# Score blocks issued one step later, norm factors spread by rounded products of ones, low diagonals on ScalarE in two places, second latent sum inside the next slab

## The reference, cut to what matters

```python
def rms_norm_2(x, g):
    y = xf * lax.rsqrt(jnp.mean(xf * xf, axis=-1, keepdims=True) + EPS)
    return (y * g.astype(jnp.float32)).astype(x.dtype)

def hgrn2_recurrence(q, k, v, log_f):
    ...
    b = jnp.cumsum(log_f, axis=3)
    q_in = q * jnp.exp(b)
    k_in = k * jnp.exp(-b)
    k_out = k * jnp.exp(b_last - b)
    scores = jnp.einsum('nbhtk,nbhsk->nbhts', q_in, k_in)
    scores = jnp.where(causal, scores, 0.0)
    o_intra = jnp.einsum('nbhts,nbhsv->nbhtv', scores, v)
    def step(state, inp):
        q_n, k_n, v_n, dec_n = inp
        o_inter = jnp.einsum('bhtk,bhkv->bhtv', q_n, state)
        state = state * dec_n[..., None] + jnp.einsum('bhsk,bhsv->bhkv', k_n, v_n)
        return state, o_inter
    ...

def hgrn2_branch(hq, hf, hi, hz, lb, hg_norm_g):
    f = lb + (1.0 - lb) * jax.nn.sigmoid(hf.astype(jnp.float32))
    q = jax.nn.silu(hq.astype(jnp.float32)).reshape(B, S, HG_HEADS, HG_DIM)
    ...
    o = rms_norm_2(o, hg_norm_g)
    o = o * jax.nn.silu(hz).reshape(B, S, HG_HEADS, HG_DIM)
    return o.reshape(B, S, HG_WIDTH)

def mla_branch(cq, ckv, kr, mz, q_a_g, w_uq, kv_a_g, w_ukv):
    q = (rms_norm_2(cq, q_a_g) @ w_uq).reshape(B, S, MLA_HEADS, QK_DIM)
    ...
    kv = (rms_norm_2(ckv, kv_a_g) @ w_ukv).reshape(B, S, MLA_HEADS, QK_NOPE + V_DIM)
    ...
```

## Time and profile before

| | |
|---|---|
| median of 3 runs | 1286.68 us |
| the profiled execution | 1286.33 us |
| its span | 1284.5 us |
| TensorE busy | 1272.7 us, 99% of the span |
| VectorE busy | 751.1 us, 58% |
| ScalarE busy | 692.7 us, 54% |
| GpSimd busy | 498.1 us, 39% |
| granted TensorE clock | 0.999 of full speed |

### The profile page before, as it was taken

One profiled execution on the slowest core, in us unless ns is written; L12 is line 12 of the kernel. 1 busy time (PEld: TensorE's weight loads), 2 busy tenths in 40 slices (PEclk: granted clock), 3 DMA queues, 4 the chain that ended last, 5 costly groups with the idle time before them and its releaser, 6 DMA issues.

```text
span 1284.5 us, 16123 instructions
## 1 busy us (share of the span) xinstructions
PE 1272.7 (99%) x6217; PEld 1063.7 (83%) x6217; DVE 751.1 (58%) x1361; ACT 692.7 (54%) x1047; POOL 498.1 (39%) x207
## 2 busy tenths in 40 slices
PE   9999999999999999999999999999999999999998
PEld 7888888888887888888888888888888888888886
DVE  6656556552138356565668388888757556642442
ACT  5535544542235657666447578878655545462422
POOL 4453433434444332322345633343433333234530
PEclk9999999999999999999999999999999999999999
DMA  5732232324333232332143322222223222326411
GB/s 183 268 122 94 90 98 87 98 92 164 96 102 98 76 107 78 97 98 65 58 157 112 115 82 67 81 72 78 83 82 101 84 78 75 96 94 206 163 58 66
DMA packets 42588, 132.30 MB, mean 103 GB/s; under 512 B 6992, under 2 KB 9744, under 8 KB 42000
## 3 DMA queue, kind: packets, MB, share of 16 engines
q1 hardware_dynamic: 36416, 115.36, 28.5%
q10 hardware_dynamic: 6096, 15.92, 3.5%
HBM read 124.97 MB, written 10.49 MB: 105 GB/s over the span
## 4 chain that ended last, share of the span: by engine, by line
PE 83%; DVE 8%; ACT 6%; issue 2%; DMA 1%; POOL 0%; SPq 0%; ACTq 0%; DVEq 0%
PE banks L516 25%; PE banks L518 25%; PE banks L517 25%; PE banks L723 2%; PE banks L715 1%; PE banks L704 1%; ACT whi L1113 1%; DVE hd L2017 1%; DVE ylo L1783 1%; PE banks L630 1%; DMA raw<-w 1%; DVE hs L1984 1%; PE banks L965 1%; DVE nfull L1779 1%; ACT L1403 0%
## 5 line engine op out<-in xcount | busy, mean ns | idle before, releaser
L506 POOL TENSOR_TENSOR wlo<-raw,whi 128x1024 fp32r<-128x1024 f32 (+2 forms) x198 | 487.1, 2462 | 714.4 <-ACT whi L1113 714.2
L516 PE MATMUL banks<-hhi,whi 128*128 128x512 f32 x736 | 293.6, 399 | 0.2 <-DVE hlo L1830 0.2
L518 PE MATMUL banks<-hlo,whi 128*128 128x512 f32 x736 | 287.4, 390 | 0.0
L517 PE MATMUL banks<-hhi,wlo 128*128 128x512 f32 x736 | 287.1, 390 | 0.0
L1113 ACT ACTIVATE whi<-raw 128x1024 fp32r<-128x1024 f32 (+2 forms) x198 | 205.3, 1037 | 144.3 <-PE banks L518 77.7
L516 PE MATMUL banks<-yhi,whi 128*128 128x512 f32 x432 | 170.6, 395 | 0.2 <-DVE ylo L1783 0.2
L518 PE MATMUL banks<-ylo,whi 128*128 128x512 f32 x432 | 168.3, 390 | 0.0
L517 PE MATMUL banks<-yhi,wlo 128*128 128x512 f32 x432 | 168.2, 389 | 0.0
L518 PEld LDWEIGHTS banks<-hlo,whi 128*128 128x128 f32 x736 | 138.2, 188 | 30.0
L516 PEld LDWEIGHTS banks<-hhi,whi 128*128 128x128 f32 x736 | 138.3, 188 | 26.0 <-DVE hlo L1830 1.0
L517 PEld LDWEIGHTS banks<-hhi,wlo 128*128 128x128 f32 x736 | 138.6, 188 | 24.7
(11 more groups left out here) (407 smaller groups left out, 2258.6 us busy)
## 6 DMA issues: line engine op xcount, KB each, us to landing
raw<-w SPq DMA_DIRECT2D x193, 512.0 KB, 3.6
rel_tab<-relx ACTq DMA_DIRECT2D x1, 4096.0 KB, 20.1
tab<-rel_tab SPq DMA_DIRECT2D x16, 224.0 KB, 3.5
x<-xt ACTq DMA_DIRECT2D x1, 2048.0 KB, 9.3
x_kept<-x ACTq DMA_DIRECT2D x1, 2048.0 KB, 7.3
parts_kept<-mcg SPq DMA_DIRECT2D x8, 256.0 KB, 4.4
mgt<-parts_kept SPq DMA_DIRECT2D x8, 256.0 KB, 3.9
x<-x_kept ACTq DMA_DIRECT2D x1, 2048.0 KB, 10.5
```

What stands on the lines that cost most here:

```text
L506: nc.gpsimd.tensor_tensor(lo[:, begin:width], raw[:, n % 2, begin:width], f32(hi[:, begin:width]), ALU.subtract).then_inc(lo_done, 1)
L516: nc.tensor.matmul(dst, a[0], b[0], start=first, stop=False)
L517: nc.tensor.matmul(dst, a[1], b[0], start=False, stop=False)
L518: return nc.tensor.matmul(dst, a[0], b[1], start=False, stop=last)
```

## The change

The matrix of ones is kept once, rounded (`wones`). A factor is split into a high and a low part (`fhi`, `flo`), each makes a diagonal (`split_diagonal`), and TensorE multiplies `wones` by both, two float32r products in place of one float32 product. The diagonals are written into tiles that are free at that time. In the attention's norm and the second block's norm ScalarE makes the low diagonal in four instructions (`low_diagonal`); elsewhere VectorE does. For the latents the second pair of products moves into the pa slab that follows, and the low half of the rotated keys to the end of VectorE's part. In the recurrence the score blocks 1 and half of 3 are issued one step later (k 6 in place of 5), block 0 too (7 in place of 6); the product `hqb` moves behind `hg_sum` on VectorE, and its high half (`hg_scaled`) behind `hg_low` and the cut on ScalarE.

```diff
@@ norms
+            def split_diagonal(done, factor, hi, lo=None):
+                n = factor.shape[1]
+                V.tensor_copy(fhi[:, 0:n], factor).then_inc(done.did("rhi"), 1)
+                dve.wait_ge(done.sem, done.at("rhi"))
+                V.tensor_tensor(flo[:, 0:n], factor, f32(fhi[:, 0:n]), ALU.subtract).then_inc(done.did("rlo"), 1)
+                diagonal(hi, f32(fhi[:, 0:n])).then_inc(done.did("diag"), 1)
+                if lo is not None:
+                    dve.wait_ge(done.sem, done.at("rlo"))
+                    diagonal(lo, flo[:, 0:n]).then_inc(done.did("diaglo"), 1)
...
+            def low_diagonal(to):
+                for t in range(TT):
+                    last = nc.scalar.activation(to[:, t * P:(t + 1) * P], ident, ACT.Copy, scale=flo[:, t:t + 1])
+                return last
...
@@ TensorE, attention's norm (the others alike)
-                            nc.tensor.matmul(bank[3], ones, adiag, start=True, stop=True).then_inc(nbP.did("wide"), 1)
+                            nc.tensor.matmul(bank[3], wones[:, :], yhi[:, AH - 1, :], start=True, stop=False)
+                            pe.wait_ge(nbA.sem, nbA.at("diaglo"))
+                            nc.tensor.matmul(bank[3], wones[:, :], ylo[:, AH - 1, :], start=False,
+                                             stop=True).then_inc(nbP.did("wide"), 1)
@@ TensorE, latents
-            pe.wait_ge(dnV.sem, dnV.at("diag"))
-            nc.tensor.matmul(bank[3], ones, ddiag[:, 0, :], start=True, stop=True)
-            pe.wait_ge(dnV.sem, dnV.at("sum"))
-            nc.tensor.matmul(bank[5], ones, ddiag[:, 1, :], start=True, stop=True).then_inc(dnP.did("wide"), 1)
+            pe.wait_ge(dnV.sem, dnV.at("diaglo"))
+            nc.tensor.matmul(bank[3], wones[:, :], lhi[:, QL, :], start=True, stop=False)
+            nc.tensor.matmul(bank[3], wones[:, :], llo[:, QL, :], start=False, stop=True).then_inc(dnP.did("wide0"), 1)
+            def second_wide(k):
+                if k == 1:
+                    pe.wait_ge(dnV.sem, dnV.at("cross3"))
...
@@ TensorE, score blocks
-                if k == 5:
+                if k == 6:
                     pe.wait_ge(hpV.sem, hpV.at("qlo", s))
...
                     hg_block(s, 1)
                     hg_block(s, 3, slice(CROSS, CROSS + P))
-                if k == 6:
+                if k == 7:
                     if s >= 1:
                         pe.wait_ge(hoV.sem, hoV.at("sum", s - 1))
                     hg_block(s, 0)
-                if k == 7:
                     hg_block(s, 3, slice(0, CROSS))
@@ ScalarE
+            def hg_scaled(r):
                 act.wait_ge(hpV.sem, hpV.at("qb", r))
                 nc.scalar.activation(hqbs[:, r % 2, :, 0, :], hqb[:, :, :], ACT.Copy).then_inc(hpA.did("qbhi"), 1)
...
                 if u >= 0:
                     hg_low(u)
-                cut()
+                    cut()
+                    hg_scaled(s)
+                else:
+                    cut()
                 if s >= 0:
                     hg_silu_z(s)
@@ VectorE
-                V.tensor_tensor(hqb[:, :, :].rearrange("p b (c i) -> p b c i", i=HC), qin[:, 1:TT],
-                                spread(hfac[:, 1:TT, 0:4].unsqueeze(3), (TT - 1, HB, HC)),
-                                ALU.mult).then_inc(hpV.did("qb"), 1)
...
                 if r >= 1:
                     hg_sum(r - 1)
+                V.tensor_tensor(hqb[:, :, :].rearrange("p b (c i) -> p b c i", i=HC), qin[:, 1:TT],
+                                spread(hfac[:, 1:TT, 0:4].unsqueeze(3), (TT - 1, HB, HC)),
+                                ALU.mult).then_inc(hpV.did("qb"), 1)
                 dve.wait_ge(hpA.sem, hpA.at("qbhi", r))
```

More of the change, by code:

```diff
@@ L349, in build @@
         vaA = steps("va_act", ["root"])
-        vaV = steps("va_dve", ["mask", "ones", "aggr", "eps", "inv", "shift"])
+        vaV = steps("va_dve", ["mask", "aggr", "eps", "inv", "shift"])
         uzP = steps("uz_pe", ["rows", "mix0", "mix1"], 8, prime=1)
@@ L377, in build @@
         hpV = steps("hp_dve", ["k", "b", "rest", "t12", "t03", "pairs", "mid", "three0", "three1", "four", "qin", "qend",
[L378 removed]
+                               "kout", "two", "three", "kb", "qelo", "kolo", "qlo", "qb", "qblo"], HH)
         htP = steps("ht_pe", ["kt", "scores", "u", "o"], HH)
@@ L552, in token_wide @@
                 pe.wait_ge(vA.sem, vA.at(f"gelu{TT - 1}", 0))
-                nc.tensor.matmul(bank[3], ones, r0[:, 1, :], start=True, stop=True).then_inc(proP.did("wide"), 1)
+                nc.tensor.matmul(bank[3], wones[:, :], hhi[:, KT - 1, :], start=True, stop=False)
+                pe.wait_ge(proV.sem, proV.at("diaglo"))
+                nc.tensor.matmul(bank[3], wones[:, :], hlo[:, KT - 1, :], start=False, stop=True).then_inc(proP.did("wide"), 1)
             def zero_product():
@@ L623, in _ @@
                 for g in range(2):
-                    rows = nc.tensor.matmul(bank[3][:, 0:2 * P], rones[:, :], wts[:, :, g, :], start=g == 0, stop=g == 1)
+                    rows = nc.tensor.matmul(bank[3][:, 0:2 * P], wones[:, :], wts[:, :, g, :], start=g == 0, stop=g == 1)
                 rows.then_inc(uzP.did("rows"), 1)
@@ L777, in values @@
                             pe.wait_ge(n2V.sem, n2V.at("diag"))
-                            nc.tensor.matmul(bank[3], ones, diag[:, 0, :], start=True,
+                            nc.tensor.matmul(bank[3], wones[:, :], hhi[:, KT - 1, :], start=True, stop=False)
+                        if half == 0 and k == KT - 2 and t == 1:
+                            pe.wait_ge(n2A.sem, n2A.at("diaglo"))
+                            nc.tensor.matmul(bank[3], wones[:, :], hlo[:, KT - 1, :], start=False,
                                              stop=True).then_inc(n2P.did("wide"), 1)
@@ L813, in hg_square @@
                     pe.wait_ge(htA.sem, htA.at("z", u + 1))
-                nc.tensor.matmul(sum_bank(u), hones[:, :], hsqhi[:, :], start=True, stop=False)
-                nc.tensor.matmul(sum_bank(u), hones[:, :], hsqlo[:, :], start=False, stop=True).then_inc(hoP.did("ms"), 1)
+                nc.tensor.matmul(sum_bank(u), wones[:, :], hsqhi[:, :], start=True, stop=False)
+                nc.tensor.matmul(sum_bank(u), wones[:, :], hsqlo[:, :], start=False, stop=True).then_inc(hoP.did("ms"), 1)
             def hg_scores(r, k):
@@ L1001, in _ @@
             slab("g0", 0, bank[7], h)
-            pe.wait_ge(dnV.sem, dnV.at("diag"))
-            nc.tensor.matmul(bank[3], ones, ddiag[:, 0, :], start=True, stop=True)
-            pe.wait_ge(dnV.sem, dnV.at("sum"))
-            nc.tensor.matmul(bank[5], ones, ddiag[:, 1, :], start=True, stop=True).then_inc(dnP.did("wide"), 1)
+            pe.wait_ge(dnV.sem, dnV.at("diaglo"))
[4 more added lines that the diff above has]
+                    pe.wait_ge(dnV.sem, dnV.at("cross3"))
+                    nc.tensor.matmul(bank[5], wones[:, :], lhi[:, QL + 1, :], start=True, stop=False)
+                    nc.tensor.matmul(bank[5], wones[:, :], llo[:, QL + 1, :], start=False,
+                                     stop=True).then_inc(dnP.did("wide1"), 1)
             pe.wait_ge(mcA.sem, mcA.at("gate", 0))
             pe.wait_ge(hoV.sem, hoV.all())
-            slab("pa", 0, bank[7], head_out)
+            slab("pa", 0, bank[7], head_out, between=second_wide)
             for r in range(MH):
@@ L1521, in _ @@
             gate0(0)
[L1522 to L1525, removed]
             for g, b in enumerate((3, 5)):
+                act.wait_ge(dnP.sem, dnP.at(f"wide{g}"))
                 nc.scalar.activation(wides[:, g, :], bank[b], ACT.Copy).then_inc(dnA.did(f"wide{g}"), 1)
+                if g == 0:
+                    cut()
             for t in range(QL + KL):
```

68 lines of the change are left out of this document (37 added, 31 removed).

## The result

The changed kernel takes 1306.56 us (median of 5 runs, 1305.35 to 1307.41) against 1286.68 before: ratio 1.0154, 95% interval 1.0139 to 1.0169. The profiled execution took 1306.56 us, 20.23 more than that of before.

What follows compares the result with a forecast made beforehand. TensorE, 99% busy, bounds the kernel, but a ScalarE-VectorE ring sets the recurrence's rounds. 1286.33 + 19.7 (moved product) - 1.2 - 0.3 (products of ones) - 1.1 (latent low halves) = 1303.4 us; range 1291 to 1309.

Steps and rivals of the forecast that it cites:

- The ring: In the recurrence a slackless ScalarE, VectorE, ScalarE chain sets the 28.00 us round, so a ScalarE delay returns whole every round.
- The moved product: Recurrence: `hqb` behind `hg_sum` waits for GpSimd and its copy follows late; 2.9 us a round, seven rounds, +19.7 us.
- Score blocks: Recurrence, TensorE: the same matmuls issued one step later give nothing of their own.
- Products of ones: Three norms: two float32r products replace one float32 product, -0.41 us each, -1.2 us; in the latents -0.3 us.
- extra instructions: Norms: VectorE's additions cost nothing, attention's norm neither gains nor loses; ScalarE's low diagonals take at most 1.3 us, covered.
- the cover for the low diagonals: Slabs behind ScalarE's low diagonals: a buffer of four cut slabs hides the delay; if gone at both places, 2.6 us.
- Latents: Behind the recurrence: -0.3 us from shorter products, limited by ScalarE's gate, and -1.1 us from removed waits for `llo`.
- The clock: Rival: TensorE's clock falls to 1.2 GHz in a new 3 us gap each round; +6.3, 1309.7 us; chance 0.06.
- a sign: Expected evidence in the recurrence: TensorE waits at the score blocks on the Silu of mz, 3 us in seven rounds.
- The sum: Whole kernel: 1286.33 + 19.7 - 1.2 - 0.3 - 1.1 = 1303.4 us.

Runs made afterwards that it cites:

- 1: Changed kernel with the product `hqb` and its high half put back in their old places; 1285.99 us, ratio 0.9989.
- 3: Kernel before with only the score blocks issued one step later; 1286.34 us, ratio 0.9995.
- 4: Changed kernel with `hqb`, its copy and the score blocks as before, leaving the norm parts alone; 1286.45 us, ratio 0.9995.
- 7: Changed kernel with `hqb` in its old place, its copy moved into ScalarE's wait for the masks, its low half behind the masks; 1281.24 us, ratio 0.9954.
- 8: As 7, with the attention norm's low diagonal made by VectorE in one instruction in place of ScalarE's four; 1281.14 us, ratio 0.9956.
- 11: Kernel before with only the copy of `hqb` moved into ScalarE's wait for the masks and its low half behind the masks; 1282.95 us, ratio 0.9970.
- 5: Changed kernel with `hqb` two places earlier on VectorE, ahead of the last low half, its copy still behind the cut; 1284.86 us, ratio 0.9983.
- 6: Changed kernel with `hqb` directly ahead of `hg_sum`, behind the last low half; 1289.43 us, ratio 1.0017.
- 9: Changed kernel with the cut ahead of `hqb`'s copy moved behind the keys' cut, so GpSimd rests while `hqb` runs; 1294.28 us, ratio 1.0058.
- 2: Kernel before with only `hqb` moved behind `hg_sum` and its high half behind the cut; 1307.20 us, ratio 1.0155.
- 10: Changed kernel with score block 0 computed four more times while TensorE waits for the Silu of mz; 1304.42 us, ratio 1.0137.
- 12: As 8, with the cut behind `hg_low` also moved into ScalarE's wait for the masks; 1280.04 us, ratio 0.9952.

## Why the prediction was right, point by point

**The ring.** Right, and all twelve experiments bear it out. Take ScalarE's time from the start of its copy of q's scaled part (`hqxhi`, 826.80 before) to the start of the table load for the Silus (829.77), beside the length of a round:

| kernel | copy to table load | round |
|---|---|---|
| before; 1; 3; 4 | 2.97; 2.98; 2.98; 2.97 | 28.00 |
| 7, 8 and 11 | 2.36 | 27.39 |
| 5 | 2.77 | 27.78 |
| 6 | 3.55 | 28.57 |
| 9 | 4.21 | 29.25 |
| 2, after, 10 | 5.79, 5.80, 5.80 | 30.82, 30.81, 30.83 |
| 12 | 1.41 | 27.08 |

In every line but the last a round is that time plus 25.03, within 0.02. In the last that sum would be 26.44, and the round is 27.08: TensorE's own work, which I had put at 27.15.

**The moved product**, the main term: 19.7 forecast, 19.1 in the ledger (20.1 at the last block less 1.0 brought in). Each round grew by 2.81, not 2.91: the time from copy to table load grew by 2.83. Its two causes, the copy's wait (1.25) and GpSimd (1.56), are parted by experiment 9.

**Score blocks.** Right: nothing of their own (3). The old wait would only have moved.

**Products of ones and extra instructions.** Here the prediction erred. It had -1.2 from three norms ahead of the recurrence; the ledger has +1.0 there. Of that, 0.25 was already there at the first product (40.78 against 40.53), so it is no part of the change; this start differs by -0.2 to +0.9 from one trace here to the next. The rest, +0.8, stands in all the traces in which ScalarE makes both low diagonals (0.7 to 0.8). The product itself gives what was worked out: two starts of 0.24 at 380.51 and 380.75 in place of 0.87. Two steps failed: "the attention's norm, where I count neither gain nor loss" (1.25 us of new waits), and the cover for the low diagonals, a "slab some steps away" (0.5 us at the second block's norm); some 0.2 more comes in steps of about 0.1 between the first norm and the attention's, and for these I have no cause. First the attention's norm. The rows of after, ScalarE, GpSimd, VectorE, then TensorE:

```profile
378.91 1.28 ACT L1278 ACTIVATE ylo<-cst,flo 128x128 fp32r<-128x128 f32 x4 [0.43 <-DVE flo L1709]
380.10 2.00 ACT L1127 ACTIVATE whi<-raw 128x1024 fp32r<-128x1024 f32 x2
...
381.22 5.24 POOL L506 TENSOR_TENSOR wlo<-raw,whi 128x1024 fp32r<-128x1024 f32 x2 [8.71 <-ACT whi L1127]
...
382.64 1.55 DVE L1827 TENSOR_TENSOR ylo<-nfull,yhi 128x512 fp32r<-128x512 f32 x1
...
384.77 2.23 DVE L1827 TENSOR_TENSOR ylo<-nfull,yhi 128x512 fp32r<-128x512 f32 x1
...
405.93 0.50 PE L516 MATMUL banks<-yhi,whi 128*128 128x512 f32 x1 [0.26 <-DVE ylo L1827]
```

and before, VectorE and GpSimd:

```profile
382.94 1.84 DVE L1783 TENSOR_TENSOR ylo<-nfull,yhi 128x512 fp32r<-128x512 f32 x1
...
379.39 4.84 POOL L506 TENSOR_TENSOR wlo<-raw,whi 128x1024 fp32r<-128x1024 f32 x2 [7.00 <-ACT whi L1113]
```

No slab was late at this norm. The four small instructions moved two cuts back by up to 1.8 us (378.27 to 380.10), so GpSimd's two slabs held up two low halves where they had held up one. The norm's third low half came 0.97 us later (387.59, before 386.62), and TensorE waits for the chain three times in place of once, 1.25 us more. It is the main term's mechanism at a second place, which I had not looked for. Experiment 8 shows that ScalarE is not the whole of it: with its cut back at 378.24, the low half that meets GpSimd takes 2.61, and GpSimd's two slabs 5.19 in place of 4.84; they start beside VectorE's second diagonal, which is my reading of the difference, not one that was tried.

At the second block's norm slabs were late, and it shows only in TensorE's weight loads (PEld), whose waits are marked, and in the matmuls with them:

```profile
680.67 2.43 POOL L506 TENSOR_TENSOR wlo<-raw,whi 128x1024 fp32r<-128x1024 f32 x1 [4.52 <-ACT whi L1127]
683.15 0.19 PEld L516 LDWEIGHTS banks<-yhi,whi 128*128 128x128 f32 x1 [0.49 <-POOL wlo L506]
683.15 0.50 PE L516 MATMUL banks<-yhi,whi 128*128 128x512 f32 x1
...
686.27 2.43 POOL L506 TENSOR_TENSOR wlo<-raw,whi 128x1024 fp32r<-128x1024 f32 x1 [3.17 <-ACT whi L1127]
688.76 0.19 PEld L516 LDWEIGHTS banks<-whi,yhi 128*128 128x128 f32 x1 [0.29 <-POOL wlo L506]
```

The second product of ones stands six slab matmuls behind the first (673.85 against 672.22), ScalarE takes its result at 674.28 in place of 672.43, and its next cut comes at 679.54 in place of 677.70; the slab made from it lands as TensorE needs it. From the product to 689.09 TensorE loses 0.5 us by it. So the buffer of four cut slabs covered a part of the delay, not all of it.

**Latents.** -1.4 forecast, -0.7 in the ledger (21.7 to 21.0). Both waits for `llo` are gone, as counted, and the gate limits the first slab, as counted (0.3 us of wait). Not counted: the first head's gating product `mcg` is late once, a gap of 0.89 at 1014.70 where before there was none. In the chain ahead of it on VectorE the small `msm` instruction of the softmax takes 1.74 us, before 0.66, with GpSimd's subtraction beside it. In experiments 7 and 10 `msm` takes 0.9 and this wait is absent, and there the same stretch gives -1.4, the whole forecast.

**The clock.** The third rival, given 0.06, was real and only its price was off. It asked for a gap of 3 us; one of 2.1 to 2.2 was enough. It took about 1.4 us (seven starts, 0.2 each) in all seven rounds; six of these vanished in the next wait, and the last one is the 1.6 between +20.1 and +21.7. I had let 0.9 of it through in each round. It is also why TensorE waits 1.9 us a round for the Silu of mz and not the 3 that the prediction gave as a sign: the slow matmuls fill the rest. The Trainium skill ("TensorE: Matmul & The Clock Gate", Part 1) says that the clock falls to 1.2 GHz when the engine idles; the changed kernel and experiment 10 agree. But the length of the gap alone does not decide: experiment 2 has gaps of 2.75 us in four rounds with the matmuls behind them 0.23 apart, and slow ones only behind its last two gaps, of 2.74 and 2.08. What decides stays open.

**The sum.** 17.1 forecast against the profiled execution, 20.2 measured. The 3.1 between them: the norms +2.2 (0.25 of it not theirs), the clock +1.6, the latents +0.7, the product -0.6, and -0.8 behind the latents. The prediction had nothing there, but 0.7 of this belongs to the change: from the matmul at 1200 us of before to the last, the ten kernels with the norm parts all gain 0.71, and the three without them (2, 3, 11) gain 0.00. Most of it comes behind 1235 us, where the matmuls stand on average some 3 ns closer together in the ten; why is open. The main term was right to 0.6; that the whole came within 3.1 is in part luck, since the misses are 4.5 us one way and 1.4 the other.

## What to carry to other kernels

Before pricing a moved instruction, close the loop: follow each engine's idle mark until you are back where you started. If no link is the busiest engine, the loop has a length of its own, what is put on it is paid in full in every round, and what is put into one of its waits is free. And look at who runs beside the new place: a VectorE instruction with two SBUF inputs is cheap or four times as dear according to whether GpSimd is at work, and a few small instructions ahead of the one that feeds GpSimd move that meeting elsewhere.

## What the runs showed of the hardware

- The order of arrival decides between VectorE and GpSimd within 0.1 us: `hqb` 2.14 us behind an instruction with a PSUM input, 0.55 directly behind one with two SBUF inputs, with GpSimd's subtraction at 2.40 and 2.82.
- TensorE's granted clock fell to 0.50, 1.2 GHz, behind gaps of 2.1 to 2.2 us in seven rounds, and did not behind four gaps of 2.75 in experiment 2, nor behind gaps of 1.6 (experiment 9) or 1.4 (experiment 10).
